# Output weights loaded by k planes, x in column halves, later lower bounds, one more round in the decayed attention

## The chip, the core and the metric

The kernel runs on one core of a Trainium2 chip. Its time is the device time of one execution in microseconds (us). Of a core's engines it uses TensorE (PE, matmuls and transposes; PEld is its weight load), VectorE (DVE), ScalarE (ACT), and SyncE (SP), which issues every transfer from HBM to SBUF. GpSimd (POOL) does nothing but four memsets. The 16 DMA engines move what SP issues.

## The reference

256 tokens of width 1024 pass two layers of a first block and one layer of a second. All is float32. Cut to what the change touches:

```python
for l in range(2):                                  # first block
    h = rms_norm(x, g_pre[l])
    u = h @ w_in[l]                                 # 3344 columns
    (qa, ka, va, ga, qb, kb, vb, gb, rb, qm, gm) = jnp.split(u, split_idx, axis=-1)
    oa = moba_attention(...) * silu(ga)             # 8 heads, columns 0 to 511 of o
    log_a = log_sigmoid(rb @ w_gate_up[l] + b) / 16
    ob = rms_norm(gla_attention(qb, kb, vb, log_a)) * silu(gb)   # decayed, columns 512 to 767
    om = mem_attention(...) * silu(gm)              # columns 768 to 1023
    x = x + jnp.concatenate([oa, ob, om], axis=-1) @ w_out[l]
# second block
lb = jnp.cumsum(jax.nn.softmax(hg_lower_bound), axis=0)
fg = lb + (1.0 - lb) * jax.nn.sigmoid(f_raw)        # f_raw: a projection of the new h
logf = jnp.log(fg)
# then HGRN2, latent attention, a mixture of 64 experts, a last norm
```

## The kernel before

A planner, `order_of_work` (L199), writes one list of steps. Each engine's function (`tensor` L1077, `scalar` L1562, `vector` L1973, `sync` L2679) walks this list in order and issues its part of each step, so the list fixes the order on every engine. An engine executes in order: an instruction that waits for a semaphore holds everything behind it.

**Projections.** A weight matrix comes as uses, each some 2 MB of HBM copied by one transfer into one of two 16 KB slots per partition (`slot_of`, u % 2). The transfer of use u waits until the last piece of use u - 2 has been rounded (`plan.ends`, `weights` L2686). A piece is one plane of 128 rows by up to 512 columns. A step "split" rounds it: ACT copies it to w_hi (fp32r), DVE writes the remainder w_lo. Six buffer pairs (`NRW`) turn round, so the split of piece q waits until the matmuls of piece q - 6 are done, and is issued about five pieces before its own. A step "mult" then runs three products (hi by hi, hi by lo, lo by hi) for each of the two 128-token tiles, usually six matmuls of 512 columns. The activations are held the same way: a step "turn" transposes two 128-column pieces of x (or o) on PE, ACT writes hT_hi (or oS_hi), DVE writes hT_lo (or oS_lo).

**The helpers.** L1577 is any copy on ACT, L1574 any other activation, L1569 a table load in front of one (L1577 for the very first). L1980, L1985, L1984 and L1988 are DVE's two-operand and scalar operations. L1107 and L1104 are the projection matmuls, L1138 the transposes of a "turn", L1087 smaller transposes.

**What interleaves.** `layer(l)` (L434) runs five generators in turn, one `yield` each: projections, softmaxes, gated, decayed and outs. A round is two pieces of the projections. `gla(l)` (L375) is the decayed attention, in two tiles of 128 tokens: decay and exp, scale (DVE, four 128x512 products), near and far (PE, L1223 and L1232; DVE's last two products stand beside near), collect (one DVE operation, seven ACT copies), cross, out (L1253), sum, root, norm. `after(n, fn)` puts a step n pieces later.

**The end of a layer.** `outs` (L514) multiplies o by w_out. w_out comes as two uses, columns 0 to 511 and columns 512 to 1023, each with all eight k planes. `BY_TURN` (L48) takes k planes 4 to 7, then 0 and 1, then 2 and 3, each for both column halves. After the last piece of a half comes "residual" (DVE adds to x), and the turns of the new x, both of the first half after the last matmul of the layer. The first mult of the next projection needs the first turn.

**Lower bounds.** "bounds" stands six pieces after the gate projection of layer 1: DVE subtracts (128x1024), ACT takes a sigmoid (128x1024, its own table), DVE makes 1 - lb. "f out" of the second block, a sigmoid too, and "forget" (DVE, three 128x512 operations a tile, L1980 and L1985), "turn f" (L1087) follow its first projection.

**The start.** SP issues x (1 MB), the identity (first 128 columns of cst), the packed gains pk, then the first weights in two halves. Every "turn" on PE waits for identity and pk together.

Of the kernel before, what the change touches and what calls it, by code (L numbers as in the profile page):

```python
# [6 lines left out]
F32 = mybir.dt.float32  # L7
# [41 lines left out]
NRW = 6  # L49
# [117 lines left out]
def streams(A):  # L167


    def rows(w):  # L170
        return w.rearrange("(k p) n -> p k n", p=128)

    out = []
    for l in range(2):
        w = rows(A["w_in"][l])
        for q in ORDER[l]:
            if q in COLS:
                out.append(("split", w[:, :, COLS[q][0]:COLS[q][1]], 8, COLS[q][1] - COLS[q][0], None))
# [12 lines left out]
    for n in ("w_branch_hgrn_2", "w_branch_mla_2"):  # L191
        for c0 in (0, 512):
            out.append(("split", rows(A[n][0])[:, :, c0:c0 + 512], 8, 512, None))
    for k in (0, 4):
        out.append(("fold", rows(A["w_out_2"][0])[:, k:k + 4, :], 4, 1024, None))
    return out


def order_of_work(uses):  # L199
# [8 lines left out]
    for u, (kind, _, k, n, _) in enumerate(uses):  # L208
        if kind == "split":
            parts += [(u, q, n, None) for q in range(k)]  # L210
        elif kind == "pair":
            if uses[u - 1][0] == "pair":
                parts += [(u + h - 1, q, n, None) for ks in BY_TURN for h in range(2) for q in ks]
        elif kind == "whole":
            parts.append((u, None, n, None))
# [5 lines left out]
    def after(n, fn):  # L221

        later.append([n, fn])
# [151 lines left out]
    def gla(l):  # L375
        def tile(t):
# [10 lines left out]
            yield  # L387
            while len(P.pool) < 3:
                yield
# [44 lines left out]
    def layer(l):  # L434
# [3 lines left out]
        def projections():  # L438
# [4 lines left out]
            for q in ORDER[l]:  # L443
# [41 lines left out]
                if l == 1 and q == "ga":  # L485
                    after(6, step("bounds"))
# [27 lines left out]
        def outs():  # L514
# [6 lines left out]
            for h, k in [(h, k) for ks in BY_TURN for h in range(2) for k in ks]:  # L521
# [16 lines left out]
    for k2 in range(0, 8, 2):  # L538
        turn(0, k2, ("hT", 0, k2))
    stats(0, 2)  # L540
# [290 lines left out]
def program(nc, A, out, cap=CAP):  # L831
    with ExitStack() as ctx:
        def sem(n):
            return ctx.enter_context(nc.semaphore(n))
# [138 lines left out]
        s_cst, s_x, s_mem, s_pk = sem("s_cst"), sem("s_xl"), sem("s_ml"), sem("s_pk")  # L973
# [24 lines left out]
        def slot_of(u):  # L998
            s = 6 if u == NU - 1 else u % 2
            return slots[s][:, 0:uses[u][2] * uses[u][3]].rearrange("p (k n) -> p k n", k=uses[u][2])  # L1000

# [75 lines left out]
        def tensor(e):  # L1077
# [12 lines left out]
            for kind, *s in plan.steps:  # L1090
# [21 lines left out]
                elif kind == "turn":  # L1112
                    n, k2, B = s
                    src = turned(n, k2)[0]
                    w.wait_ge(s_pk, 32)
                    if n == 0:
                        w.wait_ge(s_x, 16)
# [444 lines left out]
        def scalar(e):  # L1562
# [37 lines left out]

            for kind, *s in plan.steps:
                if kind == "stats sum":
                    n, = s
                    if n in (0, "mem"):
                        w.wait_ge(*((s_x, 16) if n == 0 else (s_mem, 16)))
# [4 lines left out]
                elif kind == "turn":  # L1610
                    n, k2, B = s
                    w.wait_ge(s_pk, 32)
# [15 lines left out]
                elif kind == "split":  # L1628
# [6 lines left out]
                    if half is not None:  # L1635
                        o = copy(in_runs(RW[q % NRW][0][:, 0, :], 4), in_runs(slot_of(u)[:, kp, :], 8)[:, :, 4 * half:4 * half + 4])
                    else:
                        o = copy(RW[q % NRW][0][:, 0, 0:n], slot_of(u)[:, kp, :], scale=p(gain)[:, kp:kp + 1] if gain else 1.0)
# [334 lines left out]
        def vector(e):  # L1973
# [91 lines left out]
            for kind, *s in plan.steps:  # L2065
                if kind == "prepare":
                    w.wait_ge(s_pk, 32)
# [3 lines left out]
                elif kind == "stats sum":  # L2071
# [6 lines left out]
                    else:  # L2078
                        src = x if n == 0 else memx
                        w.wait_ge(*((s_x, 16) if n == 0 else (s_mem, 16)))  # L2080
# [15 lines left out]
                elif kind == "turn":  # L2096
# [3 lines left out]
                    w.wait_ge(s_pk, 32)  # L2100
# [7 lines left out]
                elif kind == "split":  # L2108
# [4 lines left out]
                    src, gain = slot_of(u)[:, kp, :], uses[u][4]  # L2113
                    if part is not None:
                        o = tt(in_runs(lo, 4), in_runs(src, 8)[:, :, 4 * part:4 * part + 4], in_runs(hi.bitcast(F32), 4), ALU.subtract)
# [218 lines left out]
                elif kind == "residual":  # L2334
                    l, half, bs = s
                    for t in range(2):
# [5 lines left out]
                        else:  # L2342
                            w.wait_ge(*(at("new x", l - 1, half, t) if l else (s_x, 16)))
# [335 lines left out]
        def sync(e):  # L2679
# [183 lines left out]
```

## Time and profile before

| | us |
|---|---|
| median of 3 runs | 1646.81 |
| lowest, highest | 1646.54, 1649.82 |
| the profiled execution, its own time | 1648.79 |
| its span, first to last instruction | 1646.8 |
| PE busy in the span | 1456.2 (88%) |
| DVE busy, ACT busy | 636.7 (39%), 507.8 (31%) |
| moved by DMA | 496.42 MB |
| mean granted TensorE clock | 0.976 |

Times in rows are us from the span's start. In the expert part, from about 700 us on, the DMA engines are busy throughout; before it PE is. PEclk is the clock granted to TensorE as a share of full speed: 1.00 is 2.4 GHz, 0.50 is 1.2 GHz. In a row of a timeline the brackets give the idle time of the engine just before the instruction and what ended it.

### The profile page before, as it was taken

The page shows a single profiled execution, that of the slowest core. Times are in us where ns is not written, and L with a number is a line of the kernel's source. Part 1 is how long each engine was busy: PE and PEld are TensorE (multiplying, and loading weights), DVE is VectorE, ACT ScalarE, POOL GpSimd, SP SyncE. Part 2 cuts the span into 40 slices and gives each one's busy share as a digit, 9 for nine tenths or more (in the row PEclk, how much of TensorE's full clock was granted, in tenths as well). Part 3 has the DMA queues.
Part 4 walks back from the last instruction along what each step waited for, and adds up shares of the span by engine and source line. Part 5 has one row for each costly group of instructions (what it writes and reads, how often), then busy time and mean ns, then how long its engine had stood idle before and what let it go on. Part 6 is the DMA issues. An engine that isn't in the chain of part 4 may idle for free.

```text
span 1646.8 us, 20663 instructions
## 1 busy us (share of the span) xinstructions
PE 1456.2 (88%) x8585; PEld 873.2 (53%) x8585; DVE 636.7 (39%) x1416; ACT 507.8 (31%) x1089; POOL 0.2 (0%) x4
## 2 busy tenths in 40 slices
PE   7989899989899999889988888888888888878876
PEld 6867777768786788744433333333333333333332
DVE  5666667655745556641221211211211212212112
ACT  6656565656644665311110110101100010101102
POOL 0000000000000000000000000000000000000000
PEclk9999999989999999989999999999999899999999
DMA  7422243343233256689999999999999999999995
GB/s 255 175 103 103 101 145 114 116 153 122 103 109 127 82 201 229 260 365 428 428 426 427 428 427 427 428 426 427 428 429 427 427 428 426 428 427 427 428 427 221
DMA packets 74452, 496.42 MB, mean 301 GB/s; under 512 B 6224, under 2 KB 10608, under 8 KB 49392
## 3 DMA queue, kind: packets, MB, share of 16 engines
q1 hardware_dynamic: 74352, 495.03, 73.8%
q8 instruction: 70, 1.15, 0.3%
q14 instruction: 30, 0.25, 0.0%
HBM read 493.96 MB, written 1.05 MB: 301 GB/s over the span
## 4 chain that ended last, share of the span: by engine, by line
PE 47%; DMA 41%; DVE 6%; ACT 4%; issue 1%; SPq 0%; DVEq 0%; ACTq 0%
DMA arena<-in_expert_w 40%; PE ps L1107 20%; PE ps L1450 5%; PE ps L1457 3%; PE ps L1471 3%; DVE arena L1980 3%; PE ps L1482 3%; PE ps L1104 2%; ACT arena L1577 1%; DVE w_lo L1980 1%; ACT arena L1574 1%; PE ps L1203 1%; PE ps L1087 1%; PE ps L1434 1%; DMA arena<-in_w_in 1%
## 5 line engine op out<-in xcount | busy, mean ns | idle before, releaser
L1450 PE MATMUL ps<-arena 128*32 128x512 f32 x2048 | 252.0, 611 | 118.9 <-DMA arena<-in_expert_w 118.8
L1977 DVE COPY arena<-ps 128x512 f32<-128x512 f32 (+2 forms) x203 | 114.7, 588 | 529.8 <-PE ps L1450 426.4
L1577 ACT ACTIVATE arena<-ps 128x512 f32<-128x512 f32 (+6 forms) x244 | 121.5, 500 | 558.4 <-PE ps L1471 274.2
L1980 DVE TENSOR_TENSOR w_lo<-arena,w_hi 128x512 fp32r<-128x512 f32 (+2 forms) x304 | 200.1, 672 | 151.4 <-ACT w_hi L1577 150.3
L1457 PE MATMUL ps<-arena 128*128 128x512 f32 x512 | 255.1, 621 | 0.0
L1577 ACT ACTIVATE w_hi<-arena 128x512 fp32r<-128x512 f32 (+2 forms) x320 | 193.0, 621 | 115.1 <-PE ps L1107 95.4
L1450 PEld LDWEIGHTS ps<-arena 128*32 128x32 f32 x2048 | 54.1, 110 | 267.5 <-DMA arena<-in_expert_w 176.4
L1107 PE MATMUL ps<-w_hi,hT_hi 128*128 128x512 f32 (+3 forms) x448 | 178.5, 398 | 9.6 <-DVE w_lo L1980 3.8
L1482 PEld LDWEIGHTS ps<-arena 128*128 128x128 f32 x1024 | 130.9, 194 | 88.7 <-issue 84.9
L1107 PE MATMUL ps<-w_hi,hT_lo 128*128 128x512 f32 (+3 forms) x448 | 168.4, 376 | 0.0
L1107 PE MATMUL ps<-w_lo,hT_hi 128*128 128x512 f32 (+3 forms) x448 | 168.1, 375 | 0.0
L1574 ACT ACTIVATE arena<-ps 128x128 f32<-128x128 f32 (+2 forms) x140 | 48.6, 372 | 340.1 <-PE ps L1482 320.2
L1457 PEld LDWEIGHTS ps<-arena 128*128 128x128 f32 x512 | 88.2, 192 | 118.6 <-issue 118.6
L1482 PE MATMUL ps<-arena 128*128 128x32 f32 x1024 | 133.2, 274 | 3.5 <-DVE arena L1977 3.1
L1471 PE MATMUL ps<-arena 128*32 128x512 f32 x1024 | 127.6, 617 | 1.4 <-DMA arena<-in_expert_w 0.4
L1980 DVE TENSOR_TENSOR arena<-arena,ps 128x128 f32<-128x128 f32 (+1 forms) x84 | 32.9, 398 | 196.5 <-PE ps L1482 187.7
L1107 PEld LDWEIGHTS ps<-w_hi,hT_hi 128*128 128x128 f32 x448 | 86.0, 192 | 34.1 <-issue 11.9
L1107 PEld LDWEIGHTS ps<-w_hi,hT_lo 128*128 128x128 f32 x448 | 85.9, 192 | 15.0
L1107 PEld LDWEIGHTS ps<-w_lo,hT_hi 128*128 128x128 f32 x448 | 86.3, 193 | 12.4 <-issue 0.7
L1980 DVE TENSOR_TENSOR arena<-arena 128x512 f32<-128x512 f32 (+7 forms) x191 | 74.0, 404 | 12.1 <-ACT arena L1574 7.9
L1574 ACT ACTIVATE arena<-arena 128x128 f32<-128x128 f32 (+7 forms) x132 | 52.1, 399 | 67.4 <-DVE arena L1980 40.9
L1471 PEld LDWEIGHTS ps<-arena 128*32 128x32 f32 x1024 | 27.3, 111 | 51.6 <-issue 41.1
(153 smaller groups left out, 1416.2 us busy)
## 6 DMA issues: line engine op xcount, KB each, us to landing
arena<-in_expert_w SPq DMA_DIRECT2D x191, 2048.0 KB, 31.7
arena<-in_w_in SPq DMA_DIRECT2D x24, 2048.0 KB, 7.8
arena<-in_w_out SPq DMA_DIRECT2D x6, 2048.0 KB, 7.9
arena<-in_w_mem_kv SPq DMA_DIRECT2D x2, 2048.0 KB, 11.9
arena<-in_w_branch_hgrn SPq DMA_DIRECT2D x2, 2048.0 KB, 7.9
arena<-in_w_branch_mla SPq DMA_DIRECT2D x2, 2048.0 KB, 7.8
arena<-in_w_in SPq DMA_DIRECT2D x2, 1536.0 KB, 6.5
arena<-in_mla_w_uq SPq DMA_DIRECT2D x2, 1152.0 KB, 5.6
```

Source lines behind the costliest of these rows:

```text
L1087: i = e.transpose(ps(B)[:, j * 128:j * 128 + 128], src[:, j * 128:j * 128 + 128], ident)
L1104: i = e.matmul(ps(B)[:, o:o + 256], wp[:, 0, c0:c0 + 128], hp, start=st, stop=en, skip_group_check=True)
L1107: i = e.matmul(ps(B)[:, o:o + n], hp[:, t * 128:t * 128 + 128], wp[:, 0, c0:c0 + n], start=st, stop=en, skip_group_check=True)
L1203: o = e.matmul(ps(B)[:, j * dv:j * dv + dv], T[:, c0 + kt * 128:c0 + kt * 128 + 128], val[:, kt, i * dv:i * dv + dv], start=kt == 0, stop= ...
L1450: o = e.matmul(B[32 * j:32 * j + 32, :], Xs[:, k, q:q + 32], Wn[:, k, :], start=i == 0, stop=i == 1)
L1457: i = e.matmul(acc[t][h][:, :], CT[ex % 2][:, t * 128:t * 128 + 128], Ys[:, h * 512:h * 512 + 512], start=ex == 0, stop=ex == NE - 1)
L1471: i = e.matmul(B[32 * j:32 * j + 32, :], hid[ex % 2][:, 32 * j:32 * j + 32], W2[:, j, h * 512:h * 512 + 512], start=True, stop=True)
L1482: i = e.matmul(B6[:, 128 * h + 32 * j:128 * h + 32 * j + 32], (H1s, H3s)[h][:, j * 128:j * 128 + 128], c("S4"), start=True, stop=True)
L1574: return e.activation(o, i, f, scale=scale, **more)
L1577: return e.activation(o, i, ACTF.Copy, scale=scale)
L1977: return e.tensor_copy(o, i)
L1980: return e.tensor_tensor(o, a, b, op)
```

## The change

Six edits, all of order; no arithmetic is added or removed.

1. w_out comes as k planes 4 to 7, then k planes 0 to 3, each with all 1024 columns. The order of the products stays, so the first use is used up after 8 pieces (it was 14), and the second is first read at piece 9 (it was 5).
2. x comes in two column halves, each with its own semaphore. The identity is first and has a semaphore of its own, pk stands between the halves. PE's turns no longer wait for pk.
3. The exp and log table is loaded at the start of ACT's program, before any wait.
4. The first two weight pieces are split between the first turns.
5. `gla` has one more `yield` between scale and near. All that follows in both tiles stands a round later, and tile 1 starts later.
6. The first turn of the new x stands one piece earlier (all before: `2 + k2 % 4 // 2 * h`), and "bounds" stands six pieces into the second block instead of in layer 1.

```diff
-        for c0 in (0, 512):
-            out.append(("pair", rows(A["w_out"][l])[:, :, c0:c0 + 512], 8, 512, None))
+        for k in (4, 0):
+            out.append(("pair", rows(A["w_out"][l])[:, k:k + 4, :], 4, 1024, None))
...
             add("gla scale", l, t, E, K, Q)
             yield
+            yield
...
-                if l == 1 and q == "ga":
-                    after(6, step("bounds"))
...
                     for k2 in (4 * h, 4 * h + 2):
-                        after(2 + k2 % 4 // 2 * h, lambda k2=k2: turn(l + 1, k2, ("hT", l + 1, k2)))
+                        after(1 + h + k2 % 4 // 2, lambda k2=k2: turn(l + 1, k2, ("hT", l + 1, k2)))
...
             stats(l + 1, 2)
+            if l == 1:
+                after(6, step("bounds"))
...
     for k2 in range(0, 8, 2):
         turn(0, k2, ("hT", 0, k2))
+        if k2 < 4:
+            prepare()
...
-            e.dma_start(x, A["x"].rearrange("a (t p) d -> p (a t) d", p=128)).then_inc(s_x, 16)
-            e.dma_start(cst[:, 0:128], A["cst"][:, 0:128]).then_inc(s_pk, 16)
-            e.dma_start(pk, A["pk"]).then_inc(s_pk, 16)
+            e.dma_start(cst[:, 0:128], A["cst"][:, 0:128]).then_inc(s_id, 16)
+            for h in range(2):
+                cs = slice(h * 512, h * 512 + 512)
+                e.dma_start(x[:, :, cs], A["x"].rearrange("a (t p) d -> p (a t) d", p=128)[:, :, cs]).then_inc(s_x[h], 16)
+                if h == 0:
+                    e.dma_start(pk, A["pk"]).then_inc(s_pk, 16)
```

ACT at the program's start, before and after: the table load, the hi parts of x (hT_hi) and of the first weights (w_hi).

```order
L1577 ACT_TABLE_LOAD
L1577 ACTIVATE hT_hi<-ps,arena 128x256 x8
L1577 ACTIVATE w_hi_53<-arena 128x384
L1577 ACTIVATE w_hi_55<-arena 128x384
L1577 ACTIVATE w_hi_57<-arena 128x384
```

```order
L1580 ACT_TABLE_LOAD
L1588 ACTIVATE hT_hi<-ps,arena 128x256 x2
L1588 ACTIVATE w_hi_53<-arena 128x384
L1588 ACTIVATE hT_hi<-ps,arena 128x256 x2
L1588 ACTIVATE w_hi_55<-arena 128x384
L1588 ACTIVATE hT_hi<-ps,arena 128x256 x4
L1588 ACTIVATE w_hi_57<-arena 128x384
```

The first weight piece now stands behind two hT_hi copies where it stood behind eight.

ACT in layer 0 where the memory queries are taken out of PSUM, before and after. The seven small copies (16x4x16, 32x4x32, 64x4x64) are collect of tile 0; the table load, the 128x64 and the next four activations are the first sine, the gate silu and the squares; 128x512 and 128x128 are exp of tile 1.

```order
L1577 ACTIVATE arena<-ps 16x4x16 x4
L1577 ACTIVATE arena<-ps 32x4x32 x2
L1577 ACTIVATE arena<-ps 64x4x64
L1577 ACTIVATE w_hi_55<-arena 128x512
L1577 ACTIVATE w_hi_57<-arena 128x512
L1569 ACT_TABLE_LOAD
L1574 ACTIVATE arena<-arena 128x64
L1574 ACTIVATE arena<-ps,arena 128x256 x2
L1574 ACTIVATE arena<-ps 128x256 x2
L1569 ACT_TABLE_LOAD
L1574 ACTIVATE arena<-ps 128x512
L1574 ACTIVATE arena<-ps 128x128 x2
```

```order
L1588 ACTIVATE w_hi_55<-arena 128x512
L1588 ACTIVATE w_hi_57<-arena 128x512
L1580 ACT_TABLE_LOAD
L1585 ACTIVATE arena<-arena 128x64
L1585 ACTIVATE arena<-ps,arena 128x256 x2
L1585 ACTIVATE arena<-ps 128x256 x2
L1588 ACTIVATE arena<-ps 16x4x16 x4
L1588 ACTIVATE arena<-ps 32x4x32 x2
L1588 ACTIVATE arena<-ps 64x4x64
L1588 ACTIVATE w_hi_59<-arena 128x512
L1588 ACTIVATE w_hi_61<-arena 128x512
L1580 ACT_TABLE_LOAD
```

Collect now stands behind the squares, and exp of tile 1 two pairs of w_hi later.

ACT in the first projection of the second block, before and after: 128x1024 is the sigmoid of "bounds", 128x512 x2 is "f out".

```order
L1577 ACTIVATE w_hi_57<-arena 128x512
L1577 ACTIVATE w_hi_59<-arena 128x512
L1577 ACTIVATE w_hi_61<-arena 128x512
L1569 ACT_TABLE_LOAD
L1574 ACTIVATE arena<-ps,arena 128x512 x2
```

```order
L1588 ACTIVATE w_hi_57<-arena 128x512
L1580 ACT_TABLE_LOAD
L1585 ACTIVATE arena<-arena 128x1024
L1588 ACTIVATE w_hi_59<-arena 128x512
L1588 ACTIVATE w_hi_61<-arena 128x512
L1585 ACTIVATE arena<-ps,arena 128x512 x2
```

"bounds" now stands in front of two w_hi and "f out"; one table load serves both sigmoids.

## Rows read from the trace of the kernel before

**Rows 1.** The page, section 2: busy tenths in 40 slices of 41 us.

```profile
PE   7989899989899999889988888888888888878876
DMA  7422243343233256689999999999999999999995
```

**Rows 2.** Windows: stretch, its length, busy us and count of each engine, PEclk, DMA, GB/s.

```profile
63.50:69.00 5.50, 5.50 (x26) 4.53 (x25) 4.81 (x9) 3.35 (x7) 0.00 (x0) 1.00 0.00 0
14.00:19.80 5.80, 5.74 (x27) 5.74 (x28) 4.75 (x12) 3.98 (x8) 0.00 (x0) 0.50 1.06 403
88.50:94.90 6.40, 6.37 (x20) 3.84 (x21) 6.23 (x16) 1.53 (x4) 0.00 (x0) 0.50 0.56 190
187.70:190.40 2.70, 2.68 (x6) 2.16 (x7) 0.34 (x1) 0.00 (x0) 0.00 (x0) 0.50 1.05 408
245.10:248.60 3.50, 3.50 (x16) 2.72 (x9) 3.33 (x11) 0.34 (x3) 0.00 (x0) 0.52 0.55 165
334.40:340.70 6.30, 6.25 (x20) 5.29 (x21) 3.21 (x8) 2.62 (x5) 0.00 (x0) 0.50 0.29 81
347.60:350.80 3.20, 3.17 (x8) 2.52 (x9) 0.47 (x1) 0.28 (x1) 0.00 (x0) 0.51 1.03 392
```

**Rows 3.** Waits of PE over the span: us in total, times, longest.

```profile
PE ps L1138 <- DMA arena<-in_pk: 6.9, 1, 6.9
PE ps L1223 <- DVE arena L1980: 6.5, 2, 3.9
...
PE ps L1107 <- DVE oS_lo L1980: 5.1, 2, 2.8
...
PE ps L1107 <- DVE w_lo L1980: 3.8, 1, 3.8
...
PE ps L1107 <- DVE hT_lo L1988: 3.0, 2, 1.5
PE ps L1087 <- ACT arena L1574: 2.9, 2, 2.5
...
PE ps L1164 <- ACT arena L1577: 2.1, 2, 1.6
```

**Rows 4.** DMA issues of the first 30 us: KB each, median us to landing.

```profile
arena<-in_w_in SPq DMA_DIRECT2D x2, 768.0 KB, 7.6
...
arena<-in_pk SPq DMA_DIRECT2D x1, 206.5 KB, 5.2
```

**Rows 5.** Timeline of ACT, then of DVE, at the start.

```profile
9.44 3.03 ACT L1577 ACTIVATE hT_hi<-ps,arena 128x256 fp32r<-128x256 f32 x8
12.31 2.63 ACT L1577 ACTIVATE w_hi<-arena 128x384 fp32r<-128x384 f32 x6
...
13.46 2.89 DVE L1980 TENSOR_TENSOR w_lo<-arena,w_hi 128x384 fp32r<-128x384 f32 x6
```

**Rows 6.** Timeline of ACT: collect of tile 0, layer 0.

```profile
74.99 1.85 ACT L1577 ACTIVATE arena<-ps 16x64 f32<-16x64 f32 x7 [2.46 <-DVE arena L1980]
```

**Rows 7.** Timeline of ACT, then of DVE, at the end of layer 0.

```profile
185.84 0.52 ACT L1577 ACTIVATE w_hi<-arena 128x384 fp32r<-128x384 f32 x1 [4.12 <-DMA arena<-in_w_in]
...
197.73 1.27 DVE L1980 TENSOR_TENSOR arena<-arena,ps 128x512 f32<-128x512 f32 x2
```

**Rows 8.** Timelines of DVE and ACT around "bounds", layer 1.

```profile
328.12 1.22 DVE L1980 TENSOR_TENSOR arena<-arena 128x1024 f32<-128x1024 f32 x1
...
329.37 1.28 ACT L1569 ACT_TABLE_LOAD   x1 [1.88 <-DVE arena L1980]
...
331.75 0.69 DVE L1985 TENSOR_SCALAR arena<-arena 128x1024 f32<-128x1024 f32 x1 [2.41 <-ACT arena L1574]
```

**Rows 9.** Timelines of DVE, ACT and PE in the second block's first projections.

```profile
365.81 1.29 DVE L1980 TENSOR_TENSOR w_lo<-arena,w_hi 128x512 fp32r<-128x512 f32 x2
...
370.02 1.27 ACT L1574 ACTIVATE arena<-ps,arena 128x512 f32<-128x512 f32 x2
...
374.38 0.66 PE L1087 MATMUL ps<-arena 128*128 128x128 f32 x4 [0.90 <-DVE arena L1985]
```

More of the change, by code:

```diff
@@ L211, in order_of_work @@
         elif kind == "pair":
-            if uses[u - 1][0] == "pair":
-                parts += [(u + h - 1, q, n, None) for ks in BY_TURN for h in range(2) for q in ks]
+            parts += [(u, q % 4, 512, h) for ks in (BY_TURN[1:] if uses[u - 1][0] == "pair" else BY_TURN[:1])
+                      for h in range(2) for q in ks]
         elif kind == "whole":
@@ L972, in program @@
         ident = c("ident")
-        s_cst, s_x, s_mem, s_pk = sem("s_cst"), sem("s_xl"), sem("s_ml"), sem("s_pk")
+        s_cst, s_mem, s_id, s_pk = sem("s_cst"), sem("s_ml"), sem("s_id"), sem("s_pk")
+        s_x = [sem("s_xl0"), sem("s_xl1")]
         s_first = [sem("s_first0"), sem("s_first1")]
@@ L1000, in slot_of, with columns @@
             return slots[s][:, 0:uses[u][2] * uses[u][3]].rearrange("p (k n) -> p k n", k=uses[u][2])
+        def columns(u, k, half):
+            plane = slot_of(u)[:, k, :]
+            if uses[u][0] == "fold":
+                return in_runs(plane, 8)[:, :, 4 * half:4 * half + 4]
+            return plane if half is None else plane[:, 512 * half:512 * half + 512]
         def landed(u, k=0):
@@ L1114, in tensor @@
                     src = turned(n, k2)[0]
-                    w.wait_ge(s_pk, 32)
+                    w.wait_ge(s_id, 16)
                     if n == 0:
-                        w.wait_ge(s_x, 16)
+                        w.wait_ge(s_x[k2 // 4], 16)
                     elif n == "mem":
@@ L1599, in squared @@
                 run(o, i, ACTF.Square).then_inc(mark(act_norm, ("squared", *key)), 1)
+            use(EXP_LN)
             for kind, *s in plan.steps:
@@ L1604, in scalar @@
                     if n in (0, "mem"):
-                        w.wait_ge(*((s_x, 16) if n == 0 else (s_mem, 16)))
+                        for arrived in (s_x if n == 0 else [s_mem]):
+                            w.wait_ge(arrived, 16)
                         run(oG[:, 0, :], (x if n == 0 else memx)[:, 0, :], ACTF.Square, accum_out=SS[n][:, 0:1]).then_inc(
@@ L1611, in scalar @@
                     n, k2, B = s
-                    w.wait_ge(s_pk, 32)
+                    w.wait_ge(s_pk, 16)
                     w.wait_ge(*at("in", *B))
@@ L1634, in scalar @@
                     gain = uses[u][4]
[L1635 to L1638, printed above, removed]
+                    hi, src = RW[q % NRW][0][:, 0, 0:n], columns(u, kp, half)
+                    if uses[u][0] == "fold":
+                        hi = in_runs(hi, 4)
+                    o = copy(hi, src, scale=p(gain)[:, kp:kp + 1] if gain else 1.0)
                     o.then_inc(mark(act_hi, ("hi", q)), 1)
@@ L2066, in vector @@
                 if kind == "prepare":
-                    w.wait_ge(s_pk, 32)
+                    w.wait_ge(s_pk, 16)
                     for (what, l), o in g8.items():
@@ L2079, in vector @@
                         src = x if n == 0 else memx
-                        w.wait_ge(*((s_x, 16) if n == 0 else (s_mem, 16)))
+                        for arrived in (s_x if n == 0 else [s_mem]):
+                            w.wait_ge(arrived, 16)
                         e.tensor_tensor_reduce(oG[:, 1, :], src[:, 1, :], src[:, 1, :], 1.0, 0.0, ALU.mult, ALU.add,
@@ L2112, in vector @@
                     w.wait_ge(*at("hi", q))
-                    src, gain = slot_of(u)[:, kp, :], uses[u][4]
-                    if part is not None:
-                        o = tt(in_runs(lo, 4), in_runs(src, 8)[:, :, 4 * part:4 * part + 4], in_runs(hi.bitcast(F32), 4), ALU.subtract)
+                    src, gain = columns(u, kp, part), uses[u][4]
+                    if uses[u][0] == "fold":
+                        o = tt(in_runs(lo, 4), src, in_runs(hi.bitcast(F32), 4), ALU.subtract)
                     elif gain:
@@ L2342, in vector @@
                         else:
-                            w.wait_ge(*(at("new x", l - 1, half, t) if l else (s_x, 16)))
+                            w.wait_ge(*(at("new x", l - 1, half, t) if l else (s_x[half], 16)))
                         tt(o, o, i, ALU.add).then_inc(mark(dve_out, ("new x", l, half, t), ("outV", *bs[t])), 1)
```

2 lines of the change are left out of this document (1 added, 1 removed).

## The prediction

> **What bounds the kernel now.** I read the page first, then the waits of PE, then the windows. The page [rows 1] shows two parts: up to about 700 us PE is busy nearly all the time and the DMA engines a third of it, after that the DMA engines are at nine tenths in every slice. All edits lie in the first 380 us. There PE is the bound, so only two things can be won: time in which PE waits, and time in which it runs at the lower clock. What is won moves the start of the expert part by the same amount, because its transfers wait for the end of earlier work and not for a clock of their own; its length does not change. So the gain is a sum over PE's waits.
>
> The waits that the edits can touch are few [rows 3]: 6.9 us for pk and 3.8 us for the first w_lo, both before 14.1 us; 6.5 us in two waits at near (L1223); 5.1 us in two for oS_lo; 3.0 us in two for hT_lo; 2.5 us of the 2.9 us at L1087 for an exp; 2.1 us in two at the memory scores (L1164). The reader should see in the windows [rows 2] what a wait costs beyond itself: at full clock PE starts 26 matmuls in 5.5 us, and after the waits at near, oS_lo and the exp the granted clock is 0.50, the lower of its two levels (1.2 GHz), for 6.4, 3.5, 2.7, 3.2 and 6.3 us. Half of each such stretch is lost. After the two waits for hT_lo, 1.5 us each, no such stretch follows.
>
> **The start.** PE's first weight matmul begins when the first w_lo is done: DVE starts it at 13.46, ACT's w_hi at 12.31, because eight hT_hi copies from 9.44 on (3.03 us) stand in front of it, and they began only after 16 transposes had started at 6.9 and a table load had run [rows 3, 5]. In the new order two hT_hi copies are in front, the table is loaded while nothing has landed, and the transposes need the identity and half of x. What is late next is the landing of the first w_in half: issued at about 2.2, and the shorter of two landings whose median is 7.6, so about 9.0 [rows 4]. The bytes ahead of it are the same, so it does not move. Then w_hi 0.5, w_lo 0.55: PE starts at 10.1, which is 4.0 us sooner. The next pieces: ACT still has six hT_hi copies (0.38 each) among its w_hi (0.42 each), so w_lo of the third piece is ready at 13.6, and at the lower clock PE needs it at 13.9 (9 matmuls of 0.21 a piece [rows 2], two pieces): it fits. The stretch at the lower clock, 5.8 us long [rows 2], may be shorter since PE is idle for 1.5 us and not 3.8 before it; but ACT would then be the limit within four pieces, so I add nothing. **4.0 us**, bounds 2.7 (the first half lands a median after the later issue, at 10.3) and 5.0. The time of pk is nearly free: it landed at 6.9 with 1.3 MB ahead of and in it, now 0.8 MB.
>
> Against halving x speaks a rule. The row shows the two w_in halves of 768 KB, queued behind others, arriving while the DMA engines move 400 GB/s. The Trainium skill, DMA: Bandwidth & Descriptors, section Bandwidth, says to batch transfers to 1 MiB or more to get 75% of the peak. If that held for transfers that follow each other on one queue, the 2.1 MB up to the first half of w_in would take 1.8 us longer (an estimate from that page) and the start would give 2.2; the row speaks against it.
>
> **The extra round in the decayed attention.** Near of tile 1 waited 3.9 us in layer 0 and 2.6 us in layer 1, since DVE's scale was late behind two table loads and the squares on ACT. Now near follows scale by four pieces, not two; a piece is 1.37 us (6 matmuls at 26 in 5.5 us plus a little [rows 2]), and exp of tile 1 has left the crowded place. I replayed ACT, DVE and PE from 69 us with the durations of the rows: w_lo, scale and near are ready 1 to 2 us before PE asks. So the 6.5 us go, and the two slow stretches behind them, (6.4 + 3.5) / 2 = 4.95. New waits take the place of a part: collect of tile 0 (1.85 us on ACT [rows 6]) now stands behind a table load, the sine and the squares, and out of tile 0 follows two pieces after it, not four. The replay gives a wait of 0.5 us in layer 0 and 0.2 in layer 1, which has no sine. The memory scores wait 2.1 us in all now; of this about 0.9 go, since ACT reaches their operands sooner, and 0.2 more may come at the first softmax transposes. 6.5 + 4.95 - 0.7 + 0.9 - 0.2 = **11.5 us**, bounds 5 (the new waits as long as the old ones without slow stretches) and 13.
>
> **Output weights by k planes.** At 185.84 ACT had waited 4.1 us for in_w_in [rows 7]: the next layer's first weights could be fetched only once both column halves of w_out were nearly used up. oS_hi stands behind this in ACT's queue, so PE waited 2.8 us (and 2.4 in layer 1). Now the slot is free six pieces earlier, about 8 us, and the 4.1 us are covered with 4 to spare. What is late next is the chain itself: transposes, oS_hi, oS_lo, PE. With nothing in front this chain is the same as that of hT_lo, 1.5 us. So the waits shrink from 5.1 to 3.0, and as 1.5 us of idle left the clock up before, the slow stretches go: (2.7 + 3.2) / 2 = 2.95. **5.0 us**, bounds 2 and 7. The second use of w_out is read later than before, so it cannot be late; SP's issue of the lower bounds waits for ob of layer 1, now some 14 pieces later, but still 10 pieces ahead of the w_in transfer that stands behind it.
>
> **First turn of the new x.** It removes 3.0 us of waits at the first mult. But residual of the second half (DVE, from 197.73 [rows 7]) stands behind the second hT_lo pair, which now starts as late as before, and the third turn needs it. In layer 0 (a piece is 9 short matmuls) PE then waits about 0.9 at that turn and gives back most; in layer 1, with 1.37 us a piece, 0.4. **1.3 us**, bounds 0 and 3.
>
> **Lower bounds.** In layer 1, DVE is held for 1.22 + 2.41 + 0.69 us, ACT loads two tables [rows 8], and PE waits 2.5 us for an exp, then runs 6.3 us at the lower clock: 2.5 + 3.15 = 5.65 go (the same place in layer 0, without "bounds", has no wait). In the new place DVE starts at 367.1, behind the two w_lo [rows 9]; the subtraction ends at 368.3, load and sigmoid (1.28 and 1.06) at 370.7, two w_hi at 371.7. f out started at 370.02 before, so forget and turn f come 1.7 us later. PE already waited 0.90 there [rows 9], so it now waits 2.6, long enough for a slow stretch as after the waits of 2.4 to 2.8: 1.35 to 3.15 lost, I take 1.7. The second turn f no longer waits (0.3). 5.65 - 1.7 - 1.7 + 0.3 = **2.5 us**, bounds 0 and 5. The w_lo pieces held by DVE have four pieces of cover, 5.5 us against 4.3.
>
> The table load rows cost 1.28 us and the next activation starts at once [rows 8]. The Trainium skill, ScalarE: Activation LUTs, section What ACT_TABLE_LOAD costs, puts a switch at 2.66 us with a drain. No drain shows here; by the page this term would be about 1 us larger.
>
> **Sum.** 4.0 + 11.5 + 5.0 + 1.3 + 2.5 = 24.3 us. The profiled execution took 1648.79 us for a span of 1646.8; 24.3 less is 1624.5. The median of before is 1646.81, 2.0 below that execution, and the forecast is made against the median: **1622.5 us**.
>
> **Rivals.**
> - *A wait takes the place of near.* ACT, which carries collect, squares and two copies of w_hi in one round, becomes the late one: out of tile 0 waits 3 us in each layer and drags a slow stretch of 3 us (1.5 lost). For it: ACT was the cause of the present wait. Against it: ACT is busy 3.35 of 5.5 us at 63.5 [rows 2]. The term falls from 11.5 to about 3.5: 1630.5.
> - *"bounds" costs more than it frees.* The wait at turn f becomes 4 us with a slow stretch of 6.3: 5.65 - 3.1 - 3.15 - 0 = -0.6, and the start gives only 2.7: 24.3 - 3.1 - 1.3 = 19.9, 1626.9.
> - *The start and near give their full bounds* (clock up sooner): 27.5, 1619.3.
> - *Slower.* The granted clock. PE runs denser after the change; if it fell to its lower level for a long stretch between 100 and 640 us, half the stretch is lost. It must last over 50 us to cancel the sum, some 60 to be slower by 0.2%: about 1652. The longest such stretch now is 6.4 us, and it follows idle time [rows 2], so this is unlikely. It would end slower than before.
> - *It does not do what it says*: waits remain because a transfer, not the order, was late. Near and bounds wait for engines, only w_out for a transfer. Within 0.2%: 1646.
>
> **How the numbers follow.** Sum as forecast, with its own spread of 4 us: 0.50, 1622.5. Near replaced: 0.18, 1630.5. Bounds and start poor: 0.12, 1627. Full bounds: 0.10, 1619. Same: 0.06. Slower: 0.04. The likeliest sets the prediction. The range 1615 to 1634 leaves out same, slower and the tails. Of the first four cases nearly all is over 0.2% (3.3 us, about what a measurement of this kernel can tell from no change): faster 0.90, same 0.06, slower 0.04.
>
> **What would show it.** In the profile after: first weight matmul at about 10 us; no wait at L1223; a new short one at out (L1253); oS_lo waits of 1.5 and no wait of ACT for in_w_in before 360 us; hT_lo waits gone, and a short wait of the third turn (L1138) instead; the 2.5 us exp wait gone; turn f waiting 2 to 3 us. The slow windows at 88, 187, 245, 334 and 347 should be at 1.00. Wrong would be: new waits over 2 us at out, cross or the softmax steps, or a first matmul after 12 us.

## The result and the profile after

| us | median | lowest to highest | ratio to the kernel before, 95% interval |
|---|---|---|---|
| before, same comparison | 1647.56 | 1646.54 to 1649.82 (4 runs) | |
| changed | 1636.38 | 1636.10 to 1638.43 (4 runs) | 0.9933 [0.9916, 0.9950] |

The changed kernel is faster by 11 us (8 to 14 by the interval), where 24.3 was forecast; the time lies outside the range, 2.4 us above its upper end. The profiled execution took 1636.1 us, its span is 1634.1 (12.7 shorter), its mean granted clock 0.979.

In this kernel the helper lines have moved by 11 to 14: projections L1118 and L1115, turns L1149, small transposes L1098, memory scores L1175, near L1234, out L1264, decay L1158. The page, section 2, against [rows 1]:

```profile
PE   7999999989999999889988988888888988888786
DMA  7422342334233256789999999999999999999995
```

The picture is the same, and the end of it too: from the end of PE's wait of 3.9 us ahead of the expert part to the end of the span it was 950.4 us before and is 950.5 now. All 12.8 us lie before 400 us. PE's waits up to 400 us, in us, times and longest, against [rows 3]:

```profile
PE ps L1149 <- DMA arena<-in_x: 6.2, 1, 6.2
PE ps L1175 <- ACT arena L1585: 5.0, 4, 1.6
PE ps L1158 <- DVE arena L1990: 3.5, 1, 3.5
PE ps L1118 <- DVE oS_lo L1993: 3.0, 2, 1.5
PE ps L1098 <- DVE arena L1998: 3.0, 1, 3.0
PE ps L1118 <- DVE w_lo L1993: 2.1, 3, 1.3
...
PE ps L1118 <- DVE hT_lo L2001: 0.8, 2, 0.5
...
PE ps L1149 <- DVE arena L1993: 0.4, 1, 0.4
...
PE ps L1264 <- ACT arena L1588: 0.3, 1, 0.3
```

Every wait that was to go is gone or about as short as forecast: near, oS_lo 1.5 twice, hT_lo (3.0 to 0.8), the exp, a short one at out. Two rows were not forecast: 3.5 us at the decay matmuls (before 0.17), and 5.0 at the memory scores (before 2.1, forecast 1.2). Windows (stretch, length, busy us of PE, PEld, DVE, ACT, POOL, PEclk, DMA, GB/s), against [rows 2]:

```profile
15.00:19.00 4.00, 4.00 (x34) 4.00 (x35) 3.57 (x9) 2.24 (x6) 0.00 (x0) 1.00 1.06 390
29.60:34.60 5.00, 5.00 (x16) 3.99 (x17) 3.25 (x10) 4.11 (x9) 0.00 (x0) 0.66 0.01 2
103.50:107.50 4.00, 4.00 (x16) 2.60 (x17) 2.85 (x5) 1.00 (x5) 0.00 (x0) 0.78 0.95 328
186.00:190.00 4.00, 4.00 (x21) 3.27 (x21) 2.18 (x4) 2.74 (x8) 0.00 (x0) 1.00 0.64 241
253.60:257.60 4.00, 3.96 (x15) 2.62 (x16) 2.89 (x5) 0.97 (x5) 0.00 (x0) 0.79 0.97 333
360.50:364.50 4.00, 4.00 (x16) 3.15 (x17) 3.29 (x6) 2.76 (x6) 0.00 (x0) 0.66 0.02 4
```

The old stretches at the lower clock (the start, 88, 187, 245, 334, 347) are gone; new ones stand behind the new waits, at 30, 105, 256, 361, and one at 430. To count them I cut each trace into windows of 1 us up to 640 us and added what is missing from 1.00. A stretch then costs 1.7 or 3.4 us. Sums: 15.4 us before, 8.5 after, 6.9 less. PE's waits up to the expert part are 41.3 us in sum before and 33.0 after, 8.3 less. Together that is more than the 12.8 us, so the two counts overlap: before, the lower clock was there while PE was still idle (PEclk 0.50 and no matmul from 13.20 to 14.06), and cost nothing. How the 12.8 us divide is not known better than that.

Where the two chains part at the start is DVE's queue. After, then before, timelines of DVE:

```profile
27.00 0.74 DVE L2001 SCALAR_TENSOR_TENSOR w_lo<-arena,w_hi 128x512 fp32r<-128x512 f32 x1
27.66 1.22 DVE L2095 CUSTOM_DVE_ANT_0 arena<-arena 128x1024 f32<-128x1024 f32 x1
28.80 0.08 DVE L2095 DVE_READ_ACCUMULATOR2_ANT arena<- 128x1 f32 x1
28.99 0.24 DVE L1998 TENSOR_SCALAR arena<-arena 128x2 f32<-128x2 f32 x2
29.14 0.41 DVE L1990 COPY arena<-ps 16x256 f32<-16x256 f32 x1
```

```profile
28.25 1.22 DVE L2081 CUSTOM_DVE_ANT_0 arena<-arena 128x1024 f32<-128x1024 f32 x1
...
29.72 0.40 DVE L1977 COPY arena<-ps 16x256 f32<-16x256 f32 x1
```

The 16x256 copy is rb, the gate bottleneck that the decay matmuls read. It came only 0.6 us sooner, behind the squares of mem (the 1.22 us row) and a queue of w_lo and mT_lo that begins in both kernels at 21 us. In the changed kernel ACT waited 1.7 us for mem_kv, until 20.3, before it could feed that queue; before, mem_kv landed at about 19.1 (issued at 5.30, 13.8 us to landing) and ACT came to it at 20.5, behind a table load. PE, which was 3.9 us ahead at the turns of mem (17.16 against 21.07), stood 3.47 us and lost 1.7 at the lower clock:

```profile
29.59 0.59 PE L1158 MATMUL ps<-arena 16*128 16x128 f32 x3 [3.47 <-DVE arena L1990]
```

### The profile page after: what moved, and what is told of

Same layout as the page of the kernel before. It is cut to its first block, busy times and chain, and to the rows that moved or that the text cites. A ratio compares the mean times of both kernels' runs of the same rounds, so it can differ in the third digit from the quotient of the medians.

```text
span 1634.1 us, 20659 instructions
## 1 busy us (share of the span) xinstructions
PE 1451.1 (89%) x8585; PEld 868.8 (53%) x8585; DVE 636.8 (39%) x1416; ACT 503.8 (31%) x1086; POOL 0.2 (0%) x4
## 4 chain that ended last, share of the span: by engine, by line
PE 45%; DMA 41%; DVE 8%; ACT 5%; issue 1%; SPq 0%; DVEq 0%; ACTq 0%
DMA arena<-in_expert_w 40%; PE ps L1118 18%; PE ps L1461 5%; PE ps L1468 3%; DVE arena L1993 3%; PE ps L1482 3%; PE ps L1493 3%; PE ps L1115 2%; ACT arena L1585 2%; DVE w_lo L1993 2%; ACT arena L1588 1%; ACT w_hi L1588 1%; PE ps L1214 1%; PE ps L1445 1%; DMA arena<-in_w_mem_kv 1%
## 5 line engine op out<-in xcount | busy, mean ns | idle before, releaser
L1588 ACT ACTIVATE arena<-ps 128x512 f32<-128x512 f32 (+5 forms) x244 | 121.7, 501 | 555.1 <-PE ps L1482 272.4
L1118 PE MATMUL ps<-w_hi,hT_hi 128*128 128x512 f32 (+3 forms) x448 | 178.0, 397 | 5.8 <-DVE w_lo L1993 2.1
L1118 PE MATMUL ps<-w_hi,hT_lo 128*128 128x512 f32 (+3 forms) x448 | 168.8, 377 | 0.0
L1118 PE MATMUL ps<-w_lo,hT_hi 128*128 128x512 f32 (+3 forms) x448 | 168.2, 376 | 0.0
L1585 ACT ACTIVATE arena<-ps 128x128 f32<-128x128 f32 (+2 forms) x140 | 48.7, 373 | 342.8 <-PE ps L1493 321.7
L1118 PEld LDWEIGHTS ps<-w_hi,hT_hi 128*128 128x128 f32 x448 | 85.7, 191 | 30.4 <-issue 9.4
L1118 PEld LDWEIGHTS ps<-w_hi,hT_lo 128*128 128x128 f32 x448 | 85.6, 191 | 15.0
L1118 PEld LDWEIGHTS ps<-w_lo,hT_hi 128*128 128x128 f32 x448 | 85.6, 191 | 12.7 <-issue 0.7
L1993 DVE TENSOR_TENSOR arena<-arena 128x512 f32<-128x512 f32 (+7 forms) x191 | 73.9, 405 | 13.1 <-ACT arena L1585 7.9
L1585 ACT ACTIVATE arena<-arena 128x128 f32<-128x128 f32 (+7 forms) x132 | 52.4, 401 | 74.4 <-DVE arena L1993 40.6
```

The costliest lines, as they stand in the source:

```text
L1118: i = e.matmul(ps(B)[:, o:o + n], hp[:, t * 128:t * 128 + 128], wp[:, 0, c0:c0 + n], start=st, stop=en, skip_group_check=True)
L1585: return e.activation(o, i, f, scale=scale, **more)
L1588: return e.activation(o, i, ACTF.Copy, scale=scale)
L1993: return e.tensor_tensor(o, a, b, op)
```

## The experiments

Four kernels with one part of the change alone, on the kernel before; then the changed kernel mended or undone in one place. The "us" are differences of medians or ratios times 1647; "stretches" is the sum of clock lost in a kernel's trace.

**Start alone** (all edits in the queue of loads, the table load and `prepare()`; nothing else).

```diff
     for k2 in range(0, 8, 2):
         turn(0, k2, ("hT", 0, k2))
+        if k2 < 4:
+            prepare()
```

> The kernel before with the start of the changed kernel alone: identity and halves of x in front, table loaded at once, two first roundings between the turns. The forecast said a gain of 4.0 us. Theory now: DVE copies the gate bottleneck (rb) only behind the second squares of mem, which wait for the landing of the first mem_kv weights at about 20 us; the 3.9 us won by 17 us are lost again at the decay matmuls (3.5 us of idle and a stretch at 0.50 behind it). It should then be 0.5 to 1.5 us SLOWER than before, with the decay starting at 29.6. Rival: the loss belongs to the combination with other edits, and alone the start gains 3 to 4 us, with the decay at 26.5.

1651.1 us, ratio 1.0012 [1.0003, 1.0022]: 2 us slower, a little more than expected. Its waits have 3.4 us at the decay. The term's sign was wrong, and it is no matter of the other edits. The two traces differ by 0.6 us only (spans 1647.4 and 1646.8); that of the kernel before had the latest start of the four with the old order.

**Extra round alone** (the one added `yield`).

> The kernel before with the extra round of the decayed attention alone (one line). The forecast said 11.5 us. Theory: the round gives about 5 us (3 in the first layer, 2 in the second), because near of tile 1 now holds its two banks while the memory scores start: the third score gets the bank that the second just left and waits for its exp, the fourth the bank of the third. Waits of about 1.6 and 0.9 us at the memory scores in each layer, a stretch at 0.50 behind the first. Rival: those waits come from the other edits (ACT shifted by the start), and this kernel gains 9 us or more with no wait over 1 us at the scores.

1643.3 us, 0.9967 [0.9954, 0.9979]: 5.4 us gained, not 11.5. Waits at the scores 5.0 us as in the changed kernel, none at near. Stretches 8.5 us. In layer 1 the 2.5 us wait for the exp is there as before, but no slow stretch follows it, and what that saves is mostly waited for at oS_lo, 5.1 us instead of 2.4:

```profile
341.82 0.77 PE L1108 MATMUL ps<-w_hi,oS_hi 128*128 128x512 f32 x1 [5.09 <-DVE oS_lo L1981]
```

There ACT stands 6.2 us for the next in_w_in (3.5 before).

**Output weights by k planes alone** (the hunks on w_out).

> The kernel before with the output weights fetched by k planes alone. The forecast said 5.0 us: oS_lo waits of 1.5 us instead of 2.8 and 2.4, no slow stretch behind them. Theory: the same, 4 to 5 us. Rival: waits hidden so far behind them (the third turn, the hT_lo waits) grow and leave 2 us or less.

1640.8 us, 0.9954 [0.9938, 0.9971]: 7.6 us gained. oS_lo waits 1.5 twice, and the stretches behind them (1.7 each) are gone: 2.1 + 3.4 = 5.5 us by the forecast's mechanism. Where the other 2.1 us come from is not shown. In its one trace the stretches are 5.1 us in all, with none in the first 80 us, where the kernel before lost 3.4 and where this edit changes nothing; but the median is not that trace.

**Bounds alone** (the two hunks on "bounds").

> The kernel before with the lower bounds moved beside the next projection alone. The forecast said 2.5 us (5.65 from the exp wait and the stretch behind it, less 1.7 and 1.7 at turn f, plus 0.3). Theory by the trace of the changed kernel: 2.5 to 3, turn f waits 3.0 us and a slow stretch follows. Rival: the 2.5 us wait for the exp was not due to the bounds, and it stays: then this kernel is 2 to 3 us slower than before.

1648.4 us, 0.9994 [0.9984, 1.0003]: nothing that can be measured. The exp wait fell from 2.5 to 0.4 us, but PE waits for it again at oS_lo, 4.4 us instead of 2.4:

```profile
344.55 0.77 PE L1107 MATMUL ps<-w_hi,oS_hi 128*128 128x512 f32 x1 [4.43 <-DVE oS_lo L1980]
```

There ACT stands 5.5 us for the next in_w_in (3.5 before) with oS_hi behind it: with w_out in column halves this point is set by a transfer, and the idle time saved in front of it (2.1 us) flows into the wait (2.0 more). The stretch at 334 (3.4 us) is gone too, but PE waits 2.4 us at turn f (0.9 before) and 4.2 us at the scores (2.1 before), and the rest was not taken apart.

**The changed kernel again.**

> The changed kernel itself, once more, as the base for the next three on the same chip, and for a second trace of it. Theory: waits as in its first trace to 0.2 us each; but the stretches at a granted clock of 0.50 may stand at other places, since in the six traces so far each such stretch costs 1.7 or 3.4 us and before, the k planes alone and the bounds alone differ at the start (3.4, 0 and 1.7 us lost) though nothing there was edited. Rival: the stretches are fixed by the program and stand at 30, 105, 256, 361 and 430 us again, 8.5 us lost in all.

1636.5 us (1634.7 to 1637.5), 0.9934 [0.9917, 0.9951]. The waits repeat to 0.4 us but for w_lo at the start (1.3 for 2.1), the stretches don't: 10.2 us lost, 3.4 at 29 to 36 where the first trace had 1.7, 1.7 at 114 where it had them at 105. One program loses 1.7 us more or less from one execution to another. Whether both ran on one chip is not known; the four kernels above did.

**Start mended.** Squares of mem four pieces later, decay two pieces later.

```diff
-                stats("mem", 8)
+                stats("mem", 12)
...
-                    after(2, decay)
+                    after(4 if l == 0 else 2, decay)
```

> The changed kernel with the squares of mem four pieces later and the first decay matmuls two pieces later (layer 0 only). Theory: the 3.9 us that the new start wins by 17 us were lost at the decay, where PE waited 3.5 us for DVE's copy of rb, which stood behind five w_lo and the mem squares. The wait falls under 0.5 us, and the kernel gains 3 to 5 us on the changed one (about 1631 to 1633). Rival: the landing of the mem_kv weights at 20.3 us is what binds; then PE waits for w_lo of the pieces it now reaches instead, 2 to 3 us, and the gain is under 1 us.

1631.1 us (1631.0 to 1631.5), 0.9905 [0.9888, 0.9921]: 5.4 us under the changed kernel of the same comparison. Its DVE, then PE:

```profile
27.55 0.41 DVE L1990 COPY arena<-ps 16x256 f32<-16x256 f32 x1
```

```profile
28.95 0.39 PE L1118 MATMUL ps<-w_hi,mT_lo 128*128 128x512 f32 x1
29.27 0.71 PE L1158 MATMUL ps<-arena 16*128 16x128 f32 x4
```

PE reaches the decay after two more pieces and doesn't wait; no w_lo is late instead (1.3 us at the first one, as in the changed kernel's second trace), and no stretch stands in the first 100 us.

**Extra round for tile 1 only.**

```diff
             add("gla scale", l, t, E, K, Q)
             yield
-            yield
+            if t == 1:
+                yield
```

> The changed kernel with the extra round for tile 1 only, so that near of tile 1 comes four pieces sooner and its banks are free before the memory scores. Theory: the waits at the scores (1.6 + 0.9 us in each layer, 5.0 in all) came from a bank reused while the exp before it still read it; here each score gets another bank. They fall to 2 us or less in all, near stays at 1 us or less, and the kernel gains 3 to 6 us on the changed one. Rival: the scores wait because ACT and DVE are late whatever the bank; then the waits stay near 5 us, and near of tile 1 waits again 1 to 2 us: same or slower by 2 us.

1651.3 us, 1.0027 [1.0016, 1.0039]: 14.8 us worse than the changed kernel. The scores don't wait, nor near; instead

```profile
PE ps L1099 <- DVE arena L1994: 6.8, 2, 4.1
...
PE ps L1253 <- ACT arena L1586: 6.2, 2, 3.1
```

the turn of qm (L1099) waits for DVE (scale of tile 1 stands ahead of the norm of qm), and cross (L1253) for ACT's collect. Theory and rival were both too mild. By the order of the steps it is tile 0's round that puts exp and scale of tile 1 behind the norm of qm, and with it the gain; tile 0's round alone was not tried.

**Other banks for the scores**, nothing moved.

```diff
             if i < n:
+                if a[0] == "mem" and i >= 2:
+                    P.pool.rotate(i - 1)
                 B = get()
```

> The changed kernel with nothing moved: only the PSUM banks of the third and fourth memory scores are others, those of the turn p just ahead of them, which ACT empties before the exp that the old bank waits for. Theory: the bank is the cause of the waits at the scores; from ACT's rows the third score can start 1.0 us sooner and the fourth 0.9 us sooner, in each layer: waits 5.0 down to 1.5 us or less, and without 1.6 us of idle one or both slow stretches behind them go (1.7 us each). Gain on the changed kernel 3.5 to 7 us. Rival (the second extra-round kernel, which gave each score a bank of its own, was slower): ACT and DVE are the bound of this place, and what is won at the scores is waited for at turn p, the values and the turns of q: gain under 1 us.

1633.8 us (1633.1 to 1634.0), 0.9916 [0.9900, 0.9933]: 2.8 us under 1636.5. The third score of layer 0, in the changed kernel and here:

```profile
103.48 1.13 PE L1175 MATMUL ps<-arena 64*128 64x256 f32 x4 [1.60 <-ACT arena L1585]
```

```profile
103.65 1.13 PE L1177 MATMUL ps<-arena 64*128 64x256 f32 x4 [0.69 <-ACT arena L1590]
```

The wait for the exp (L1585) is now one for a copy (L1590) that ACT makes just before it. So the bank was the cause of 0.9 us of 1.6. The fourth score waits 1.1 us still, for the copy of turn p. All four scores together wait 3.5 us, where 1.5 or less was expected. The rest is ACT's pace, and the gain lies between the theory (3.5 to 7) and the rival (under 1).

**Three mends together** (start, banks, bounds two pieces sooner as below).

> The changed kernel with the three edits together: start mended (5.4 us gained alone), bounds two pieces sooner (2.5 alone), other banks for the scores. Theory: they lie in separate stretches of a PE-bound part and add up: 1636.5 - 5.4 - 2.5 - (what the banks give alone, 3.5 to 7) = 1622 to 1625 us. Rival: what the start wins is given back later, as it was in the kernel before; then it stays above 1628.

1628.8 us (1625.4 to 1630.7), 0.9884 [0.9866, 0.9902]. Less than the sum, and outside the expected 1622 to 1625; the rival's figure fits, its reason is looked at below.

**Bounds two pieces sooner.**

```diff
             if l == 1:
-                after(6, step("bounds"))
+                after(4, step("bounds"))
```

> The changed kernel with the lower bounds two pieces sooner. Theory: the sigmoid of the bounds stands in front of f out on ACT and was ready about 2 us after the f bank; two w_lo pieces (1.3 us) are now behind it. Turn f waits 1.0 to 1.7 us instead of 3.0, with no stretch at 0.50 behind it: 1.5 to 3 us gained on the changed kernel. Rival: DVE, held 2.4 us by the sigmoid ahead of the row statistics, makes w_lo of the third piece after late: PE waits 1 us or more for a w_lo, gain 0.

1634.0 us, 0.9920 [0.9904, 0.9937]: 2.5 us under 1636.5. Turn f, in the changed kernel and here:

```profile
360.50 0.66 PE L1098 MATMUL ps<-arena 128*128 128x128 f32 x4 [2.97 <-DVE arena L1998]
```

```profile
356.34 0.50 PE L1118 MATMUL ps<-w_hi,hT_hi 128*128 128x512 f32 x1 [0.55 <-DVE w_lo L1993]
360.54 0.66 PE L1098 MATMUL ps<-arena 128*128 128x128 f32 x4 [1.19 <-DVE arena L1998]
```

**Bounds back, in the changed kernel.**

> The changed kernel with the bounds back at their old place, in front of the last attention steps of layer 1. Theory: alone the move of the bounds gave nearly nothing (0.3 us), because the 2.5 us it frees at the exp were waited for again at oS_lo (4.4 us instead of 2.4), where ACT waits for the next weights. With the k planes that gate is gone, so here the move is worth 2 to 4 us: this kernel at 1638.5 to 1640.5. Rival: the exp wait has another cause in this order, and the kernel is the same as the changed one or faster, since turn f no longer waits 3 us: 1634 to 1636.

1637.4 us (1635.3 to 1639.9), 0.9943 [0.9926, 0.9960]: the move is worth 0.8 us there, which can't be told from nothing, and not the expected 2 to 4. The exp waits 2.48 us again at 327.39, but no slow stretch follows, and turn f waits 0.90 and 0.34. The windows behind that same exp wait, here and with the k planes alone:

```profile
327.40:332.40 5.00, 5.00 (x30) 4.42 (x31) 3.52 (x10) 3.14 (x6) 0.00 (x0) 1.00 0.00 0
```

```profile
330.70:336.70 6.00, 5.96 (x34) 5.21 (x35) 4.44 (x12) 3.19 (x6) 0.00 (x0) 1.00 0.00 0
```

In [rows 2] the same wait was followed by 6.3 us at 0.50. So it is in the start alone and in the mended start alone, for 3.4 and 6.8 us; in the extra round alone it was followed by 1.00.

**Turns of the new x back, in the changed kernel.**

> The changed kernel with the turns of the new x back at their old places (2 and 2 + 0 or 1 pieces after). The forecast for this edit was 1.3 us. By the traces: hT_lo waits 3.0 us in all instead of 0.8, no wait of the third turn (0.4): 1.8 us slower than the changed kernel. Rival: the two waits of 1.5 us are each followed by a slow stretch now: 3 to 5 us slower.

1637.5 us (1636.3 to 1638.8), 0.9937 [0.9921, 0.9954]: the edit is worth 1.0 us by the medians and 0.5 by the ratios (forecast 1.3), which can't be told from nothing either. hT_lo waits 1.5 twice, turn f 2.4 instead of 3.0: by the waits alone the edit is worth 2.2 - 0.4 (third turn) - 0.6 = 1.2 us.

**What was left open.** Three more.

> The kernel before with the new start and with the mend of it (squares of mem four pieces later, decay two pieces later), nothing else. Theory: the forecast's 4.0 us for the start was a right reading of the first 17 us and missed only the copy of rb; with that out of the way it is worth 3 to 4 us, and 1 to 2 more if no slow stretch stands in the first 40 us: 1641.5 to 1644. Rival: on the kernel before a later wait (near of tile 1, oS_lo, where ACT waits for weights) takes the gain back, as it did with the bounds: under 1.5 us, above 1645.

1645.3 us, 0.9980 [0.9970, 0.9989]: 3.3 us gained over before, and 5.3 over the start alone. So the sign of the start was wrong because of rb, and with rb out of the way the term is inside its range of 2.7 to 5.

> The changed kernel with the three mends again, with more rounds. Theory: its first median of 1628.8 (1625.4 to 1630.7) held executions in which slow stretches or the expert part (952.0 us in its trace, 950.0 to 950.5 in most others) cost 2 to 5 us; the median here is 1627 to 1629. Rival: the sum of the single gains holds and the first median was high by chance: 1625 to 1626.

1628.3 us (1624.9 to 1629.9), 0.9869 [0.9852, 0.9885]. The sum of the single gains (1625.8) is not reached.

> The changed kernel with the start mended and the bounds sooner, the banks of the scores as they were. Alone the two gave 5.4 and 2.5 us, so 1628.6 if they add. Theory: 1628.5 to 1630, and the banks are worth 1 to 2 us on top (0.7 us less waiting at the scores in each layer). Rival: the banks' 2.8 us hold in full: then this kernel is at 1630.5 or more against 1627.5.

1628.9 us (1628.1 to 1629.8), 0.9881 [0.9865, 0.9897]. The banks are worth 0.6 us by the medians of one comparison, 2 by the ratios, whose intervals overlap: where the 2.2 us go that they gave before is known in part. The expert part took 951.9 us in both traces of all three mends, 950.2 in that of the two mends. Of the other 14 traces 12 show 950.0 to 950.9 and two show more, 951.5 (bounds alone) and 951.8 (extra round for tile 1). These four long ones are the only traces in which the granted clock took 11.9 us out of the stretch from 660 to 745 us; in the others it took 8.5 or 10.2. Against the two mends that is 3.4 us more of lost clock and 1.7 us more of time; why the clock was granted so there is not known. Besides, one slow stretch less was followed by a wait more: at 426 us the mended kernel waits 1.07 and 0.34 us for turn f at full clock, where the changed one runs slowly and doesn't wait.

All three mends together have the lowest median of the study: 1.3% under before, and about 8 us under the changed kernel.

## Why the prediction was wrong

The forecast gained 13.1 us too much. What failed is the start (4.0 forecast, a loss of 2.0 measured), the size of the extra round (11.5, and 5.4) and the price put on slow stretches in three terms. By part:

| part | forecast, us | alone, by the ratio | what the traces show |
|---|---|---|---|
| start | 4.0 (2.7 to 5) | -2.0 (-3.6 to -0.5) | first weight matmul 2.7 sooner, then rb 3.5 and a stretch of 1.7 |
| extra round | 11.5 (5 to 13) | 5.4 (3.5 to 7.6) | near -6.5, scores +2.9, stretches 5.1 gone, 3.4 new (and oS_lo +2.7 for a stretch of 3.4 gone) |
| k planes | 5.0 (2 to 7) | 7.6 (4.8 to 10.2) | as forecast, and stretches elsewhere |
| turns of x | 1.3 (0 to 3) | 1.0, taken out of the changed kernel | as forecast, not clear of noise |
| bounds | 2.5 (0 to 5) | 1.0 (-0.5 to 2.6); 0.8 taken out | exp -2.5, turn f +1.7 |
| sum | 24.3 | 13.0 | changed kernel: 11.2 |

Two slips stand in the sums: the terms of the first turn (3.0, 0.9, 0.4) give 1.7 and not 1.3, and the full bounds of start and near (1.0 and 1.5 more) give 26.8 and not 27.5.

**Start: the wrong step.** "ACT would then be the limit within four pieces, so I add nothing" ended the account at the fourth piece. The next release for PE that doesn't move with the start, the copy of rb, was not looked for. In the kernel before, PE waits 0.17 us for it, a wait near zero, and so in no row of the forecast. A second step was wrong too: "The bytes ahead of it are the same, so it does not move." The first half of w_in was there at 10.18 and not at 9.0, where it had been before, so the first weight matmul came 2.7 us sooner (11.36 for 14.06, forecast 10.1), which is the term's own lower bound. That PE was nevertheless 3.9 us ahead by 17 us, close to the 4.0, is in part luck of this pair of traces: the four traces with the old start have the turns of mem at 19.44 to 21.07, the thirteen with the new one at 16.95 to 18.71, 2.7 us apart in the mean. With the copy of rb out of the way the term is 3.3 us (1.8 to 4.9).

**Extra round: a mis-sized term and a wrong place.** The 6.5 us at near went, and out of tile 0 waits 0.3 as replayed. "About 0.9 go" at the memory scores was wrong: they wait 2.9 us more. The replay followed ACT, DVE and PE but not the PSUM banks. Eight of these (PE's output buffers) turn round in the order in which they come free: near of tile 1 now holds two of eight while the projection and the heads of q hold four, the third score takes the bank of the second, and the fourth that of the third. The rival "A wait takes the place of near" had the right kind (1630.5) and named out instead of the scores.

**The clock: the step that was wrong in three terms.** Slow stretches were counted as a sure price of a wait: 4.95 + 2.95 + 3.15 us of gain. The old ones did go, but of the changed kernel's 8.5 us 3.4 came behind the new waits at the scores and 1.7 behind the decay, none of it forecast, and 1.7 behind turn f, as forecast. In the bounds term the 3.15 us do not belong to the exp wait for certain: the same 2.5 us were followed by the lower clock in three kernels (before, the start alone, the mended start alone) and by full clock in three others (the extra round alone, the k planes alone, bounds back). By the waits alone the term is 2.5 - 1.7 = 0.8, and 0.8 and 1.0 were measured, neither clear of nothing.

**k planes and turns: right by mechanism.** The waits and stretches that belong to the k planes make 5.5 us, forecast 5.0; the 7.6 measured lie above the bounds of 2 to 7 (their interval reaches down to 4.8), and the difference is not explained. The turns' 1.0 is too small to confirm a size. **Bounds:** turn f was forecast at 2.6 us and waits 2.97.

**The range** held the bounds of single terms, but no row for a wait that would appear where PE came early. The misses of the start and of the round have the same sign for that reason.

## To carry to other kernels

When a stretch is made shorter, follow the freed engine to the next point where it needs something that does not move with it, and look at the waits near zero there as well as at the long ones; a pool of banks or buffers is such a point. A slow clock seen behind a wait in one trace is worth counting at its price only where several traces show it: here the same wait of 2.5 us had one behind it in three kernels and none in three others. Idle time that is saved just in front of a point that a transfer sets is waited for there (2.1 us saved, 2.0 waited) until the transfer is moved, so the order of edits matters when they are tried one at a time. A gain far ahead of such a point moves the transfer too: the mended start kept its 3.3 us.

## What the runs showed of the chip

Every stretch at the lower clock found up to 640 us cost 1.7 or 3.4 us, and the same program had some of its stretches in other places in a second execution. Before, the extra round alone, the k planes alone and the bounds alone have the same start and lost 3.4, 1.7, 0 and 1.7 us there, the last three on one chip. Waits that were followed by a stretch in one trace or another were 1.1 to 5.1 us long; the wait of 2.5 us for the exp was followed by 0.50 in three kernels and by 1.00 in three others. Slow stretches also hide waits, so that taking one away can give back less than its price: 1.4 us for turn f at 426 us, 2.7 us at oS_lo in the extra round alone.

Halving x was not free, but cost less than a rule would have it. The first half of w_in was there for ACT at 10.18, where 9.0 was forecast, and the median landing of its two halves grew from 7.6 [rows 4] to 8.3 us (issues up to 30 us, KB each, median us to landing):

```profile
arena<-in_w_in SPq DMA_DIRECT2D x2, 768.0 KB, 8.3
```

The loss is in the first transfers. Windows from 3 to 6 us, before and after (PE to POOL idle, then PEclk, DMA share, GB/s):

```profile
3.00:6.00 3.00, 0.00 (x0) 0.00 (x0) 0.00 (x0) 0.00 (x0) 0.00 (x0) 1.00 1.00 389
```

```profile
3.00:6.00 3.00, 0.00 (x0) 0.00 (x0) 0.00 (x0) 0.00 (x0) 0.00 (x0) 1.00 0.89 261
```

From 6 to 9 us both move 390 and 388 GB/s. Three microseconds at 128 GB/s less are 0.38 MB, 1.0 us of transfer at 389 GB/s by estimate, which is nearly all of the delay of 1.2. The start alone and the changed kernel's second trace show 254 and 247 GB/s there, the k planes alone 387.

PE's first weight matmul came 2.7 us sooner (14.06 to 11.36). By the rule of the Trainium skill, DMA: Bandwidth & Descriptors, section Bandwidth, it would have been 2.2, an estimate from that page; the trace lies between it and the forecast's 4.0. That section measured transfers issued from GpSimd, and here SyncE issues them; and no run here parts the size of the transfers from their order.
